# Two pairs of chunks of each FFN's gate and up product formed from seven block products

## The reference

```python
def swiglu(h, w_gate, w_up, w_down):
    return (jax.nn.silu(h @ w_gate) * (h @ w_up)) @ w_down

x = x + 0.5 * swiglu(rms_norm(x, g[0]), ffn_w_gate[i, 0], ffn_w_up[i, 0], ffn_w_down[i, 0])
```

## Time and profile before

| | |
|---|---|
| median of three runs | 1306.96 us |
| time of the profiled execution | 1307.18 us |
| its span | 1305.4 us |
| TensorE matmul busy | 1289.2 us (99%) |
| VectorE busy | 846.8 us (65%) |
| ScalarE busy | 654.5 us (50%) |
| GpSimd busy | 83.1 us (6%) |
| DMA | 256.87 MB, mean 197 GB/s |
| granted TensorE clock | 0.998 |

### The profile page before, as it was taken

The page is one execution under the profiler, slowest core; times in us unless marked ns, Lnnn a source line. Parts: engine busy times, 40 slices in busy tenths (PEclk is TensorE's granted clock), DMA queues, the critical chain, the costliest instruction groups (busy, mean ns, idle before and its releaser), DMA issues.

```text
span 1305.4 us, 17052 instructions
## 1 busy us (share of the span) xinstructions
PE 1289.2 (99%) x6249; PEld 1081.4 (83%) x6249; DVE 846.8 (65%) x929; ACT 654.5 (50%) x769; POOL 83.1 (6%) x195
## 2 busy tenths in 40 slices
PE   9999999999999999999999999999999999999997
PEld 7888889888888887888888877888888987888886
DVE  5665559876555567655556976555567887655554
ACT  6444457445444447544445865444447555544442
POOL 2000004100000002000001300000001300000000
PEclk9999999999999999999999999999999999999999
DMA  9776755446666745666663326666645551676771
GB/s 296 239 231 225 225 194 168 155 136 216 222 225 225 229 173 193 211 225 224 225 225 125 133 97 219 224 225 225 225 177 162 187 175 57 206 226 224 226 227 69
DMA packets 189563, 256.87 MB, mean 197 GB/s; under 512 B 9048, under 2 KB 151022, under 8 KB 189518
## 3 DMA queue, kind: packets, MB, share of 16 engines
q1 hardware_dynamic: 156560, 229.17, 53.3%
q10 hardware_dynamic: 32478, 26.30, 6.4%
q0 software_dynamic: 480, 0.80, 0.4%
HBM read 243.38 MB, written 12.85 MB: 196 GB/s over the span
## 4 chain that ended last, share of the span: by engine, by line
PE 96%; DVE 2%; ACT 1%; issue 0%; POOL 0%; POOLq 0%; DVEq 0%; ACTq 0%
PE ps L275 28%; PE ps L277 28%; PE ps L276 28%; PE ps L372 1%; PE ps L302 1%; PE ps L303 1%; PE ps L304 1%; DVE wl L247 1%; PE ps L1242 1%; PE ps L2972 0%; PE ps L666 0%; PE ps L281 0%; PE ps L2290 0%; PE ps L282 0%; PE ps L285 0%
## 5 line engine op out<-in xcount | busy, mean ns | idle before, releaser
L275 PE MATMUL ps<-wl,hth 128*128 128x512 f32 (+3 forms) x1256 | 490.1, 390 | 1.5 <-DVE htl L2148 0.8
L277 PE MATMUL ps<-wh,htl 128*128 128x512 f32 (+3 forms) x1256 | 485.0, 386 | 0.0
L276 PE MATMUL ps<-wh,hth 128*128 128x512 f32 (+3 forms) x1256 | 484.6, 386 | 0.0
L894 DVE TENSOR_TENSOR wl<-raw,wh 128x2048 fp32r<-128x2048 f32 x120 | 275.1, 2292 | 189.6 <-ACT wh L821 184.4
L821 ACT ACTIVATE wh<-raw 128x2048 fp32r<-128x2048 f32 x120 | 229.5, 1913 | 155.4 <-DMA bounce<-xn 114.8
L275 PEld LDWEIGHTS ps<-wl,hth 128*128 128x128 f32 x1256 | 236.1, 188 | 49.8 <-issue 2.7
L277 PEld LDWEIGHTS ps<-wh,htl 128*128 128x128 f32 x1256 | 236.0, 188 | 47.5
L276 PEld LDWEIGHTS ps<-wh,hth 128*128 128x128 f32 x1256 | 236.2, 188 | 44.8
L247 DVE TENSOR_TENSOR wl<-raw,wh 128x2048 fp32r<-128x2048 f32 (+3 forms) x94 | 207.5, 2216 | 63.1 <-ACT wh L236 62.3
L236 ACT ACTIVATE wh<-raw 128x2048 fp32r<-128x2048 f32 (+3 forms) x94 | 173.5, 1852 | 59.2 <-PE ps L277 43.9
L275 PE MATMUL ps<-wl,prod_h 128*128 128x512 f32 x400 | 156.3, 391 | 0.0
(11 more groups left out here) (423 smaller groups left out, 992.6 us busy)
## 6 DMA issues: line engine op xcount, KB each, us to landing
raw<-in_ffn_w_down SPq DMA_DIRECT2D x88, 512.0 KB, 4.0
raw<-in_ffn_w_gate SPq DMA_DIRECT2D x86, 512.0 KB, 4.1
raw<-in_ffn_w_up SPq DMA_DIRECT2D x86, 512.0 KB, 5.1
raw<-in_w_gate_up SPq DMA_DIRECT2D x44, 512.0 KB, 4.8
raw<-in_even_w_in SPq DMA_DIRECT2D x24, 512.0 KB, 4.5
bounce<-xn ACTq DMA_DIRECT2D x45, 256.0 KB, 3.1
xn<-bounce ACTq DMA_DIRECT2D x45, 256.0 KB, 5.1
raw<-in_w_down SPq DMA_DIRECT2D x22, 512.0 KB, 4.2
```

What stands on the lines that cost most here:

```text
L275: nc.tensor.matmul(o, xh, b, start=first, stop=False)
L276: nc.tensor.matmul(o, xh, a, start=False, stop=False)
L277: return nc.tensor.matmul(o, xl, a, start=False, stop=last)
L894: nc.vector.tensor_tensor(wl[:, r, :], raw[:, r, :], wh[:, r, :].bitcast(f32), ALU.subtract)\
```

## The change

Two chunks c and c+1 (3 and 4, 7 and 8) are taken as one product of 2 x 2 blocks: rows of tile 0 and tile 1, input features 0 to 511 and 512 to 1023, hidden features of chunk c and c+1. Written out that is eight block products ("quarters" of 12 matmuls). The change forms it of seven, by sums of row blocks and sums of weight blocks (Winograd's form of Strassen's scheme). So that sums of rows are of scaled rows, the rows are scaled first: TensorE spreads 1/rms with two small matmuls (`turn_first`), VectorE multiplies and mixes (`mix_rows`), and both parts of the four mixtures and of the last scaled block are made, once in each FFN (`mix_high_parts`, `mix_low_parts`).

Of the four sums of weight blocks two are made by DMA: SyncE loads two blocks of chunk c+1 into `SUM1` and `SUM3` (`load_far`), and GpSimd issues DMAs that add a second block to each in place (`ffn_pool`). VectorE makes the other two (`near_sums`, `last_sum`). Three sums are split beside the ring's slots (`sum_high_of`, `sum_low_of`), the fourth ("sum") takes the place of a ring slot. A pair's slots are b11, b21, b22, the down slot of the chunk before, and sum. ScalarE copies two block products out of PSUM (`evict`), VectorE combines them in five steps (`combine`). Chunk c+1's product comes before chunk c's, and both down products follow a and b of chunk c+2. The loops of all engines are written out, with the slots in the order of `ORDER`: a0 b0 a1 b1 d0 a2 b2 d1 b11 b21 b22 d2 sum a5 b5 d4 d3 a6 b6 d5 b11 b21 b22 d6 sum a9 b9 d8 d7 a10 b10 d9 d10, numbered from 0 on.

Below is the core of it; new tiles' addresses, semaphores and moved scratch of other stages are left out.

```diff
+        PAIRS = (3, 7)
+        ORDER = [("a", 0), ("b", 0), ("a", 1), ("b", 1), ("d", 0)]
+        waiting, c = [1], 2
+        while c < NCH - 1:
+            if c in PAIRS:
+                ORDER += [("b11", c), ("b21", c), ("b22", c), ("d", waiting.pop(0)), ("sum", c)]
+                waiting, c = [c + 1, c], c + 2
+            else:
+                ORDER += [("a", c), ("b", c)] + [("d", w) for w in waiting]
+                waiting, c = [c], c + 1
+        ORDER += [("a", c), ("b", c)] + [("d", w) for w in waiting] + [("d", c)]
+        assert len(ORDER) == FFN_SLOTS
+        PLACE = {what: i for i, what in enumerate(ORDER)}
+        TURN = [c for kind, c in ORDER if kind == "d"]
+        summed = [base[s] + PLACE["sum", g] for s, name in enumerate(PLAN) if name == "ffn" for g in PAIRS]
...
+            def load_far(sp, q, c):
+                if q > 0:
+                    sp.wait_ge(sums_used, 3 * q)
+                for half, at in ((0, SUM1), (1, SUM3)):
+                    v = arena[:, at:at + SLOT].rearrange("p (k n) -> p k n", k=4)
+                    for dst, src in gate_up(v, half, c * HC + HC):
+                        sp.dma_start(dst, src).then_inc(sum_loaded[half], 16)
...
+                for q, g in enumerate(PAIRS):
+                    if i == PAIR_LOADS[g]:
+                        sp.wait_ge(weights_used, n + 2)
+                        load_far(sp, len(PAIRS) * f + q, g)
+        def ffn_pool(pool, f, w_gate, w_up):
+            g_k, u_k = (w.rearrange("(k p) n -> p k n", p=P) for w in (w_gate, w_up))
+            for q, c in enumerate(PAIRS):
+                for j, half, c0, at in ((1, 0, (c + 1) * HC, SUM3), (0, 0, c * HC, SUM1)):
+                    pool.wait_ge(sum_loaded[j], 32 * (len(PAIRS) * f + q + 1))
+                    v = arena[:, at:at + SLOT].rearrange("p (k n) -> p k n", k=4)
+                    for i, w in enumerate((g_k, u_k)):
+                        pool.dma_start(v[:, :, i * HC:(i + 1) * HC], w[:, 4 * half:4 * half + 4, c0:c0 + HC],
+                                       accum_op=ALU.add).then_inc(sum_added[j], 16)
+        PAIR_LOADS = {g: (7 if q == 0 else PLACE["d", PAIRS[0]]) for q, g in enumerate(PAIRS)}
...
+            def turn_first():
+                pe.wait_ge(prod_ready, f * NCH + 1)
+                turn_product(0)
+                pe.wait_ge(mix_diag, f + 1)
+                for tt in range(TT):
+                    m = nc.tensor.matmul(ps[:, 1, tt * P:(tt + 1) * P], ones[:, :], diag[:, tt, :], start=True, stop=True)
+                m.then_inc(mix_row, 1)
+            def quarter(b, rows_h, rows_l, w_h, w_l, first, last):
+                for kk in range(4):
+                    w = slice(kk * 512, (kk + 1) * 512)
+                    m = product(bank(b), rows_h(kk), rows_l(kk), w_h[:, w], w_l[:, w], first and kk == 0, last and kk == 3, not first)
+                return m
...
+            def pair(c):
+                q = len(PAIRS) * f + PAIRS.index(c)
+                near = [of_tile(v, 0, 0) for v in (hth, htl)], [of_tile(v, 0, 1) for v in (hth, htl)]
+                pe.wait_ge(mix_low, f + 1)
+                pe.wait_ge(sum_low, 3 * q + 1)
+                quarter(3, *of_mix(2), *of_sum(HIGH3, SUM3), True, True).then_inc(sums_used, 1)
+                pe.wait_ge(prod_ready, f * NCH + TURN.index(c - 1) + 1)
+                quarter(0, *near[0], *of_slot("b11", c), True, True).then_inc(weights_used, 1)
+                pe.wait_ge(sum_low, 3 * q + 2)
+                quarter(2, *of_mix(0), *of_sum(HIGH1, SUM1), True, True).then_inc(sums_used, 1)
+                pe.wait_ge(evicted, 2 * q + 1)
+                quarter(0, *near[1], *of_slot("b21", c), False, True).then_inc(weights_used, 1)
+                pe.wait_ge(sum_low, 3 * q + 3)
+                quarter(1, *of_mix(1), *of_sum(HIGH2, SUM2), True, True).then_inc(sums_used, 1)
+                pe.wait_ge(evicted, 2 * q + 2)
+                quarter(2, *of_mix(3), *of_slot("b22", c), False, True).then_inc(weights_used, 1)
+                down(c - 1)
+                pe.wait_ge(combined, 5 * q + 1)
+                quarter(3, *of_mix(4), *of_slot("sum", c), False, True).then_inc(weights_used, 1)
+                pe.wait_ge(combined, 5 * q + 4)
...
+            waiting, c = [1], 2
+            while c < NCH - 1:
+                if c in PAIRS:
+                    pair(c)
+                    waiting, c = [c + 1, c], c + 2
+                else:
+                    plain(c)
+                    for w in waiting:
+                        down(w)
+                    pe.wait_ge(prod_ready, f * NCH + TURN.index(c) + 1)
+                    waiting, c = [c], c + 1
...
+            def silu(c, tiles=None):
+                for tt in tiles or product_tiles(c):
+                    if far(c):
+                        act.wait_ge(combined, 5 * pair_of(c - 1) + (4, 3)[tt])
+                    elif c in PAIRS:
+                        act.wait_ge(prod_ready, f * NCH + TURN.index(c))
+                        if tt == 1:
+                            act.wait_ge(combined, 5 * pair_of(c) + 5)
+                    else:
+                        act.wait_ge(weights_used, n + PLACE["b", c] + 1)
+                    nc.scalar.activation(silu_g[:, tt, :], product_rows(c, tt)[:, 0:HC], ACT.Silu, scale=row_scale(c, tt)).then_inc(silu_ready, 1)
...
+            def sum_high_of(c, j, high, at):
+                if j == 3:
+                    act.wait_ge(sum_ready, pair_of(c) + 1)
+                else:
+                    act.wait_ge(sum_added[2 - j], 32 * (pair_of(c) + 1))
+                nc.scalar.activation(arena_r[:, high:high + SLOT], arena[:, at:at + SLOT], ACT.Copy).then_inc(sum_high, 1)
+            def evict(c, j):
+                if j == 0:
+                    act.wait_ge(weights_used, n + PLACE["b11", c] + 1)
+                    nc.scalar.activation(near_1, bank(0), ACT.Copy, scale=rstd[:, 0:1]).then_inc(evicted, 1)
+                else:
+                    act.wait_ge(sums_used, 3 * pair_of(c) + 2)
+                    nc.scalar.activation(far_1, bank(2), ACT.Copy).then_inc(evicted, 1)
...
+            mix_high_parts()
+            move_in(1)
+            act_ahead.through(act, n + 7)
+            high(1)
+            late, c = None, 2
+            while c < NCH - 1:
+                if c in PAIRS:
+                    evict(c, 0)
+                    high(c - 1)
+                    through("d", c - 1)
+                    evict(c, 1)
+                    through("sum", c)
+                    silu(c + 1)
+                    act_ahead.through(act, n + PLACE["sum", c] + 1)
+                    move_out(c + 1)
+                    silu(c, (0,))
+                    move_in(c + 1)
+                    act_ahead.through(act, n + PLACE["sum", c] + 2)
+                    silu(c, (1,))
+                    act_ahead.through(act, n + PLACE["sum", c] + 3)
+                    high(c + 1)
+                    move_out(c)
+                    act_ahead.through(act, n + PLACE["sum", c] + 4)
+                    move_in(c)
+                    late, c = c, c + 2
+                    continue
+                pair_next = c + 1 in PAIRS
+                if pair_next:
+                    sum_high_of(c + 1, 1, HIGH3, SUM3)
+                    through("b11", c + 1)
+                    sum_high_of(c + 1, 2, HIGH1, SUM1)
+                    sum_high_of(c + 1, 3, HIGH2, SUM2)
+                elif late is None:
+                    through("a", c + 1)
+                silu(c)
+                if late is not None:
+                    high(late)
+                    through("a", c + 1)
+                    late = None
+                through(*(("b21", c + 1) if pair_next else ("b", c + 1)))
                 move_out(c)
-            act_ahead.n += 3 * (NCH - 3)
-            move_in(NCH - 2)
-            act_ahead.through(act, n + FFN_SLOTS - 2)
-            high(NCH - 2)
-            act_ahead.through(act, n + FFN_SLOTS - 1)
-            silu(n + 3 * (NCH - 1) + 1)
+                if pair_next:
+                    through("b22", c + 1)
+                move_in(c)
+                if not pair_next:
+                    through("d", c)
+                    high(c)
+                c += 1
+            silu(c)
+            if late is not None:
+                high(late)
...
+            def turned_rows():
+                dve_link(dve, nc.vector.tensor_tensor(rows_turned, hth[:, :, :].bitcast(f32), htl[:, :, :].bitcast(f32), ALU.add))
+            def mix_rows():
+                v = rows_turned
+                dve.wait_ge(mix_row, f + 1)
+                dve_link(dve, nc.vector.tensor_tensor(v, v, repeated(bank(1, T), 1, KT), ALU.mult))
+                a11, a12, a21, a22 = (v[:, 4 * half:4 * half + 4, tt * P:(tt + 1) * P] for tt in range(TT) for half in range(2))
+                nc.vector.tensor_tensor(mixed(2), a11, a21, ALU.subtract)
```

(101 more changed lines are left out.)

287 lines of the change are left out of this document (180 added, 107 removed).

## The result

The changed kernel takes 1421.49 us (median of four runs, 1417.25 to 1424.58), the kernel before 1306.82 beside it on the same chip: a ratio of 1.0875 (1.0844 to 1.0907), 115 us slower. The forecast had the sign, not the size: 1332.8, with 1385 as the upper end.

The account below looks back on a forecast made before the run. TensorE was taken to bound the kernel. In each FFN -5.14 + 3.0 + 1.0 + 1.4 + 2.0 + 2.9 = +5.2 us, five times +25.8, gave 1332.8 us; range over all 1287 to 1385.

Parts of the forecast that it names:

- with no wait 1281.5: Whole kernel: the time in us if the change caused no wait anywhere.
- VectorE is full in a pair: In each pair VectorE needs 24.97 us beside TensorE's 24.48: 0.5 us lost per pair, 1.0 in an FFN (0 to 2).
- Behind a pair: Chunk c's product, combined last, returns through DRAM 0.7 us late for each pair, 1.4 in an FFN (0 to 4).
- The first pair: Behind d1 TensorE waits for chunk 2's product, held up by SUM1's landing and ScalarE's order: 3.0 us in an FFN.
- the mixing that I costed at nothing: VectorE's mixing of rows before the first pair takes 10.3 us but ends about when d0 does: 0 to 1 us.
- 25.7 saved: TensorE: 27.2 us saved by fewer matmuls over ten pairs, less 1.5 for spreading 1/rms; 5.14 in each FFN.
- The second pair: Far loads ahead of slots 17 and 18 delay chunk 5's product: d5 waits 2.0 us, then 2.9 for chunk 6's product.
- Rival B: An accumulate costs double, delaying SUM1 and both pairs: +15.2 us in an FFN, 1383; B and D together 0.19.

Follow-up runs that it names:

- r4: r1 with three changes of order on VectorE and ScalarE, then four more; no second DMAs or second blocks; 1308.48 us (1.0009 of the kernel before).
- e2_none: The changed kernel without GpSimd's second DMAs, so two weight sums lack their second block; 1364.23 us (1.0438 of the kernel before).
- r3_timed: The whole change with three changes of order, first pair's far loads earlier, second pair's accumulates held until chunk 3's product is back; 1407.06 us (1.0769).
- r5_whole: The whole change with all orders of r4, first pair's far loads two slots earlier, second pair's held until chunk 3's product is back; 1390.67 us (1.0639).
- c2_stall_short: The kernel before, with ScalarE making the high part of chunk 0's product 9 more times in each FFN; 1317.78 us (1.0083).
- e1: The changed kernel with GpSimd's four DMAs of a pair loading plainly instead of adding; 1408.02 us (1.0773 of the kernel before).
- r1: e2_none with the second pair's far loads held until chunk 3's product is back from DRAM; 1343.97 us (1.0270 of the kernel before).
- m2_dma: DMAs alone: the product's way in, alone 2.7 us, behind eight SyncE loads 7.3, behind four accumulates 9.2, behind four plain GpSimd loads 5.5.

## Why the prediction was wrong

Held: TensorE bounds the kernel before, 120 matmuls go and 20 short ones come (6249 to 6149; the page counts four in an FFN where I had two, for 0.36 us, 1227.56 to 1227.92, where I took 0.3); with no wait 1281.5. SUM1's landing and ScalarE's order do hold up the first pair, for 0.7 to 4.1 us where I took 3.0. That this term is near is luck: in the last FFN d1 was due at 1250.3 and `SUM1` was there at 1261.3, 11 us later, where I had 4.0 (1156.64 to 1160.6). The wait is short only because d1 itself came 6.7 us late and ran at half clock. VectorE is full in a pair: I took 0.5 us for each. In r4 the first pair of the last FFN lasts from 1163.91 to 1190.44, 26.5 us for 24.48 (0.6 of it a wait for ScalarE's copy), the second 24.8. With the slots split late behind it and the small gaps r4 loses 5.4 us in an FFN (1308.5 less 1281.5, by five) where I had 1.0; by name VectorE's splits have 1.8 of it. The page's 65% hid this, and my sum left out that TensorE's next slots wait for the same engine once it is behind.

Failed, in order of size:

1. *Behind a pair: "I take 0.7 us late for each pair, 1.4 in an FFN (0 to 4)"*: ahead of d3 the wait was 5.8 to 9.4 us, ahead of d7 1.8 at most. The chain was the right one, summed with 3.1 and 5.1 us for the moves, their medians in the kernel before; in the last FFN they took 5.9 and 11.9. I had put the second pair's far loads and accumulates at this very time and charged them only to chunk 5 and to the sums, not to chunk 3's product, which travels through them.
2. *"The first pair"*: the product of chunk 1 stood in my DMA sum as 0.52 MB, and I let high(1) slip by up to 3 us, which would have left d1 without a wait. In the last FFN it slipped by 10.9: it began 5.6 us ahead of d1 before (1151.05, 1156.64) and 5.3 behind the time at which d1 was due after (1255.58, 1250.3). So d1 waited for 4.55, 6.45, 6.83, 5.71 and 6.68 us, one FFN after another. Of the 10.9 the way in has 6.3 (11.4 for 5.0, its time at that place before: 1146.03 to 1151.05), the way out 1.0, and 3.5 is its later start, behind the mixing that I costed at nothing. How much of the wait the mixing makes is not shown: e2_none, with the mixing in place, has no wait above 1 us ahead of d1, and r3_timed and r5_whole, with the mixtures moved behind, still have 4.5 to 8.6.
3. *Half clock*: no term of the sum had it. The time rose by 112.2 us in the span: 25.7 saved, 96.5 waited, which leaves 41.4. Twenty-four waits at some 0.4 to 0.5 beyond their length (c2_stall_short) would give 11. The other 30 are matmuls at 1.2 GHz: 142 matmuls of the FFNs show the longer duration of half clock, and together their followers start 30 us later than at 0.2267 each; the kernel before has two. In the last FFN the 24 of d1 took 8.4 us (1256.99 to 1265.42) and the 24 of d3 7.6 (1316.76 to 1324.35) for 5.44.
4. *"The second pair"*, 2.0 ahead of d5 and 2.9 ahead of the pair: neither wait was there, not in e2_none either, where d3 is less late.
5. Not seen at all: 6.9 us for `htl` ahead of d10 in four FFNs. The slot of d10 is split behind chunk 10's silu and multiply instead of ahead of them. In r4, which puts it back, these waits are gone.

The 115 us by runs: the add itself 13 (change to e1), its traffic 44 (e1 to e2), the far loads' place 20 (e2 to r1), the order around the pairs 36 (r1 to r4), what r4 still loses 27 (r4 to 1281.5, by name 8.8 of it VectorE's splits), and the saving of 25.7 against them. The parts are not independent: with the accumulates in place the order is worth 31 (change to r5), not 36 and 20.

Rival B had the nearest number, 1383, but mostly by luck. It put its 50 us in the waits ahead of the pairs; they were ahead of d1 and d3. Four accumulates cost half as much again in time, not double, and plain DMAs in their place still give 1408. The rule that I took from the Trainium skill for B ("Collectives: The Full Stack", the bandwidth ceiling) says, of transfers between cores, that a reducing copy halves the rate; the windows of m2_dma, 203 GB/s for 340, come near it as a rate, and the kernel shows that the rate was not what decided.

Left open: what makes up the 5.4 us that r4 still loses in an FFN, and how much of it could be had by moving splits out of a pair; that was not tried. Open too is why d3 waits longer behind plain DMAs (e1) than behind accumulates.

## What to carry to other kernels

A transfer added off the critical path is paid by whatever small transfer of the critical path is under way at that time: look at the timeline for what lands in its stretch, and price that with the queues full, not with its median. For each wait of TensorE of some 2 us or more put a range of 0.5 to 3 us on top for matmuls at half clock: here 1.81 us once cost the clock, 3.33 once did not, and 4.75 did in all five places. And where work is moved to an engine of 65%, sum it over the stretch where it lands: around a pair VectorE was at 94 to 98%, and even with all long waits gone nothing of the saving was left.
